# Expert gathers that begin per chunk of heads, dots ahead of the last selections, and a deeper ring of one-hot tiles

## The reference

```
q    = x @ w_q                       # 8 heads x 2 halves x 128
sc   = q . subkeys                   # 128 scores for each head and half
s_top, i_top = top16(sc)             # for each half
c_top, c_idx = top16(s_top[0][:,None] + s_top[1][None,:])   # 16 of 256 candidates
e1, e2  = i_top[0][c_idx // 16], i_top[1][c_idx % 16]
experts = e1 * 128 + e2              # 128 experts a token (8 heads x 16)
gates   = softmax(c_top)
h = sum_d x[d] * u_tab[experts, d]   # one row of 2048 for each token and expert
a = gates * gelu(h)
y = sum_k a[k] * v_tab[experts[k]]
```

## Time and profile before

| | |
|---|---|
| median of three runs | 2531.74 us (2524.23 to 2532.64) |
| the profiled execution's own time | 2534.31 us |
| its span, first to last instruction | 2532.5 us |
| busy share of the span | PE 70%, DVE 70%, ACT 35%, POOL 45% |
| indirect gathers L535 | 256, 2015 ns mean on POOL |
| dots L1243 | 256, 2288 ns mean |

### The profile page before, as it was taken

How to read it: one execution, slowest core, us unless ns; L and a number is a source line. 1 busy time by engine, 2 the same in 40 slices (tenths; PEclk the granted TensorE clock), 3 DMA queues, 4 the chain that set the end, 5 groups by cost and what they waited for, 6 DMA issues and landing times.

```text
span 2532.5 us, 24956 instructions
## 1 busy us (share of the span) xinstructions
PE 1760.8 (70%) x9462; PEld 1439.9 (57%) x9462; DVE 1762.5 (70%) x2424; ACT 877.8 (35%) x1369; POOL 1140.5 (45%) x484
## 2 busy tenths in 40 slices
PE   7997899899969630000130222799999999999798
PEld 6875778787769510000030222677777777777676
DVE  1066232422147799999999998798988899987714
ACT  3223122223222110000290794644444444444332
POOL 3662233335636266688777885022222222221154
PEclk9998899999979765555555555899999999999899
DMA  9997999987999398899999998299999899998547
GB/s 355 382 377 269 378 412 399 403 350 290 377 333 356 124 402 348 349 422 422 421 401 385 422 422 333 89 384 385 388 380 381 319 373 384 382 382 304 208 182 257
DMA packets 131558, 881.86 MB, mean 348 GB/s; under 512 B 18962, under 2 KB 20562, under 8 KB 55540
## 3 DMA queue, kind: packets, MB, share of 16 engines
q1 hardware_dynamic: 76148, 477.65, 49.3%
q0 software_dynamic: 55296, 402.68, 39.5%
HBM read 871.28 MB, written 141.63 MB: 400 GB/s over the span
## 4 chain that ended last, share of the span: by engine, by line
PE 37%; DVE 25%; POOL 14%; DMA 10%; issue 10%; ACT 2%; SPq 0%; POOLq 0%; ACTq 0%; DVEq 0%
POOL expert_rows L535 11%; PE psum L1427 10%; PE psum L1429 10%; PE psum L1428 10%; DVE expert_rows L1243 9%; DMA v_raw<-in_peer_v 7%; DVE v_lo L1369 2%; POOL w_lo L521 2%; DVE expert_rows L1304 2%; DMA cache_part<-in_k_parts 2%; DMA expert_rows<-in_peer_u,experts 2%; PE psum L1586 1%; DVE x_tokens L1313 1%; PE psum L1442 1%; PE psum L1443 1%
## 5 line engine op out<-in xcount | busy, mean ns | idle before, releaser
L535 POOL DMA_INDIRECT expert_rows<-in_peer_u,experts x256 | 515.9, 2015 | 187.8 <-DVE expert_rows L1243 81.4
L1243 DVE SCALAR_TENSOR_TENSOR expert_rows<-expert_rows,x_tokens 128x2048 f32<-128x2048 f32 x256 | 577.9, 2288 | 31.8 <-DMA expert_rows<-in_peer_u,experts 30.8
L521 POOL TENSOR_TENSOR w_lo<-w_raw,w_hi 128x2048 fp32r<-128x2048 f32 x80 | 371.2, 4640 | 476.8 <-ACT w_hi L566 476.7
L1427 PE MATMUL psum<-v_hi,gate_matrix_hi 128*128 128x512 f32 x1024 | 405.4, 396 | 33.7 <-DVE v_lo L1369 33.3
L809 ACT ACTIVATE v_hi<-v_raw 128x1024 fp32r<-128x1024 f32 x256 | 271.4, 1060 | 400.6 <-DMA v_raw<-in_peer_v 299.2
L1429 PE MATMUL psum<-v_hi,gate_matrix_lo 128*128 128x512 f32 x1024 | 399.8, 390 | 0.0
L1428 PE MATMUL psum<-v_lo,gate_matrix_hi 128*128 128x512 f32 x1024 | 399.7, 390 | 0.0
L1369 DVE TENSOR_TENSOR v_lo<-v_raw,v_hi 128x1024 fp32r<-128x1024 f32 x256 | 310.1, 1220 | 77.9 <-ACT v_hi L809 77.5
L566 ACT ACTIVATE w_hi<-w_raw 128x2048 fp32r<-128x2048 f32 x80 | 153.1, 1914 | 364.6 <-PE psum L1429 273.8
L1427 PEld LDWEIGHTS psum<-v_hi,gate_matrix_hi 128*128 128x128 f32 x1024 | 192.5, 188 | 97.6 <-issue 35.6
L1706 PE MATMUL psum<-one_hot_first_gated,one_hot_second 128*128 128x128 f32 x384 | 88.1, 405 | 221.5 <-ACT one_hot_first_gated L739 210.3
(11 more groups left out here) (307 smaller groups left out, 3071.3 us busy)
## 6 DMA issues: line engine op xcount, KB each, us to landing
v_raw<-in_peer_v SPq DMA_DIRECT2D x256, 512.0 KB, 7.2
out<-in_state_attn_k SPq DMA_DIRECT2D x64, 1020.0 KB, 10.7
out<-in_state_attn_v SPq DMA_DIRECT2D x64, 1020.0 KB, 11.2
w_raw<-in_w_in SPq DMA_DIRECT2D x48, 1024.0 KB, 8.6
cache_part<-in_k_parts SPq DMA_DIRECT2D x40, 1024.0 KB, 9.9
cache_part<-in_v_parts SPq DMA_DIRECT2D x40, 1024.0 KB, 12.5
w_raw<-in_w_out SPq DMA_DIRECT2D x16, 1024.0 KB, 7.0
w_raw<-in_peer_wq SPq DMA_DIRECT2D x16, 1024.0 KB, 6.5
```

Of the source, the lines that this page charges most:

```text
L521: nc.gpsimd.tensor_tensor(l_, r_, h_.bitcast(f32), ALU.subtract).then_inc(w_lo_ready, 1)
L535: pool.indirect_dma_start(ring[n % NSLOT][:, :], None, u_tab, bass.IndirectOffsetOnAxis(idx_p[:, n // PAIRS, n % PAIRS:n % PAIRS + 1], 0)) ...
L1243: V.scalar_tensor_tensor(out=g, in0=g, scalar=1.0, in1=xt[:, t, :], op0=ALU.mult, op1=ALU.mult, accum_out=hdot[:, t, j:j + 1]).then_inc(u_ ...
L1427: MM(out, lh, rh, start=start, stop=False)
```

## The change

Five things change. (1) The expert numbers of t = 1 are written by `select(1, c)`, chunk by chunk, and POOL may start a chunk's gathers when that chunk is known; `idx_ok` now counts four chunks and then t = 2. The slots are turned by three, so the first four gathers use slots 3 to 6; the fifth waits for the end of the query projection. (2) Before the loop stand three selections of each tile; `select(1, 3)` stands behind dot 8, `top_experts(0, 1)` behind dot 16, `select(2, 3)` behind dot 32, `top_experts(1, 2)` behind dot 48. (3) ACT makes the query copies. (4) PE makes a chunk's scores behind the first piece of the next chunk instead of the second. (5) In the open build both kinds of one-hot tile have four buffers, and ACT and DVE work three groups ahead instead of two.

```diff
+    emov_l = at("one_hot_first_late", [128, 2, EG, NK], f32, 184 * KB)
+    esta_l = at("one_hot_second_late", [128, 2, EG, NK], f32, 188 * KB)
...
+        slot_of = lambda n: (n + DSLOT) % NSLOT
...
+        deep = lambda g: g >= GROUPS // 2
+
+        def firsts(g):
+            return (emov_l if deep(g) and g % 4 > 1 else emov)[:, g % 2, :, :]
+
+        def seconds(g):
+            if early(g):
+                return gm[:, EG * g:EG * g + EG, :]
+            return (esta_l if deep(g) and g % 4 > 1 else esta)[:, g % 2, :, :]
+
+        def hots_free(g):
+            if g >= GROUPS // 2 + 4:
+                return g - 3
+            return GROUPS // 2 if deep(g) else g - 1
...
             for n in range(2 * PAIRS):
-                if n == 0 or n == PAIRS:
-                    pool.wait_ge(idx_ok, n // PAIRS + 1)
+                if n < PAIRS and n % (2 * TOPK) == 0:
+                    pool.wait_ge(idx_ok, n // (2 * TOPK) + 1)
+                if n == PAIRS:
+                    pool.wait_ge(idx_ok, 5)
+                if n == NSLOT - DSLOT:
+                    pool.wait_ge(w_used, 80)
                 if n >= NSLOT:
                     pool.wait_ge(u_free, n - NSLOT + 1)
-                pool.indirect_dma_start(ring[n % NSLOT][:, :], None, u_tab,
+                pool.indirect_dma_start(ring[slot_of(n)][:, :], None, u_tab,
...
+            def query_copies(c):
+                act.wait_ge(w_used, 64 + 4 * (c + 1))
+                for j in range(4):
+                    m = A(qpt[:, 4 * c + j, :], PS[:, 4 * (c % 2) + j, 0:N], ACT.Copy)
+                m.then_inc(acc_free, 1)
+
             for c in range(4):
                 for k in range(PPC):
                     if c > 0 or k > 1:
                         hi(64 + c * PPC + k, k % 2)
+                    if k == 1 and c > 0:
+                        query_copies(c - 1)
                     if k == 2 and c > 0:
                         score_copy(2 * c - 2)
                         score_copy(2 * c - 1)
+            query_copies(3)
...
             for g in range(GROUPS // 2, GROUPS):
-                if g + 2 < GROUPS and not by_dve(g + 2) and not early(g + 2):
-                    one_hots(g + 2)
+                if g + 3 < GROUPS and not by_dve(g + 3) and not early(g + 3):
+                    one_hots(g + 3)
...
                 if t == 1:
                     V.memset(mx[:, 2:3], 0.0).then_inc(ch_ok, 1)
+                    e1, e2 = (esel_p[:, 0, q, 2 * c:2 * c + 2, :].rearrange("p h k -> p (h k)") for q in range(2))
+                    V.scalar_tensor_tensor(out=idx_p[:, 0, 2 * TOPK * c:2 * TOPK * (c + 1)], in0=e1, scalar=float(NK), in1=e2,
+                                           op0=ALU.mult, op1=ALU.add).then_inc(idx_ok, 1)
...
-            query_copies(0)
             select(1, 0)
-            query_copies(1)
             select(2, 0)
             select(1, 1)
-            query_copies(2)
+            select(2, 1)
             select(1, 2)
-            query_copies(3)
-            select(1, 3)
-            top_experts(0, 1)
+            select(2, 2)
...
-            after_dot = {1: {8: lambda: select(2, 1), 24: lambda: select(2, 2), 40: lambda: select(2, 3),
-                             56: lambda: top_experts(1, 2)},
+            after_dot = {1: {8: lambda: select(1, 3), 16: lambda: top_experts(0, 1), 32: lambda: select(2, 3),
+                             48: lambda: top_experts(1, 2)},
...
-            for g in range(GROUPS // 2, GROUPS + 2):
+            for g in range(GROUPS // 2, GROUPS + 3):
                 if g < GROUPS:
                     one_hots(g)
-                if g - 2 >= GROUPS // 2 and by_dve(g - 2):
-                    build_copy(g - 2)
+                if g - 3 >= GROUPS // 2 and by_dve(g - 3):
+                    build_copy(g - 3)
...
-                    if k == 1 and c > 0:
+                    if k == 0 and c > 0:
                         pe.wait_ge(acc_free, 16 + c)
                         peer_scores(2 * c - 2)
                         peer_scores(2 * c - 1)
```

More of the change, by code:

```diff
@@ L312, in decoder_step @@
         by_dve = lambda g: g >= GROUPS * 3 // 4 and g % 4 == 3
-        def second_one_hot(g, j):
-            return gm[:, EG * g + j, :] if early(g) else esta[:, g % 2, j, :]
+        deep = lambda g: g >= GROUPS // 2
[9 more added lines that the diff above has]
+            return GROUPS // 2 if deep(g) else g - 1
         out_tile = lambda t: xd2[0:TS, :] if t == 0 else xt2[:, t - 1, :]
@@ L717, in one_hots @@
                 elif g >= 2:
-                    act.wait_ge(ab_mm, g - 1)
+                    act.wait_ge(ab_mm, hots_free(g))
                 else:
@@ L721, in one_hots @@
                 for j in range(EG):
-                    m = A(second_one_hot(g, j), iota[:, :], ACT.Abs, bias=eT[:, n, 1, c0 + j:c0 + j + 1], scale=-1.0)
+                    m = A(seconds(g)[:, j, :], iota[:, :], ACT.Abs, bias=eT[:, n, 1, c0 + j:c0 + j + 1], scale=-1.0)
                 m.then_inc(act_step, 1)
@@ L725, in one_hots @@
                 act.wait_ge(act_step, links[0])
-                v = (gm[:, EG * g:EG * g + EG, :] if early(g) else esta[:, g % 2, :, :]).rearrange("p a c -> p (a c)")
+                v = seconds(g).rearrange("p a c -> p (a c)")
                 A(v, v, ACT.Relu, bias=1.0, scale=-1.0).then_inc(es_e if early(g) else es_a, 1)
@@ L1197, in top_experts @@
                 e1, e2 = (parts[:, q, 0:hn, :].rearrange("p h k -> p (h k)") for q in range(2))
-                o = idx_d[:, :] if t == 0 else idx_p[:, t - 1, :]
-                link(V.scalar_tensor_tensor(out=o, in0=e1, scalar=float(NK), in1=e2, op0=ALU.mult, op1=ALU.add))
+                if t != 1:
+                    o = idx_d[:, :] if t == 0 else idx_p[:, t - 1, :]
+                    link(V.scalar_tensor_tensor(out=o, in0=e1, scalar=float(NK), in1=e2, op0=ALU.mult, op1=ALU.add))
+                if t == 2:
+                    V.memset(mx[:, 0:1], 0.0).then_inc(idx_ok, 1)
                 if t > 0:
-                    V.memset(mx[:, 0:1], 0.0).then_inc(idx_ok, 1)
                     V.memset(mx[:, 1:2], 0.0).then_inc(e_ok, 1)
@@ L1220, in select @@
                     V.memset(mx[:, 2:3], 0.0).then_inc(ch_ok, 1)
-            def query_copies(c):
-                dve.wait_ge(w_used, 64 + 4 * (c + 1))
-                for j in range(4):
-                    m = V.tensor_scalar(qpt[:, 4 * c + j, :], PS[:, 4 * (c % 2) + j, 0:N], 1.0, None, ALU.mult)
-                m.then_inc(acc_free, 1)
-            query_copies(0)
+                    e1, e2 = (esel_p[:, 0, q, 2 * c:2 * c + 2, :].rearrange("p h k -> p (h k)") for q in range(2))
+                    V.scalar_tensor_tensor(out=idx_p[:, 0, 2 * TOPK * c:2 * TOPK * (c + 1)], in0=e1, scalar=float(NK), in1=e2,
+                                           op0=ALU.mult, op1=ALU.add).then_inc(idx_ok, 1)
             select(1, 0)
-            query_copies(1)
             select(2, 0)
             select(1, 1)
-            query_copies(2)
+            select(2, 1)
             select(1, 2)
-            query_copies(3)
-            select(1, 3)
-            top_experts(0, 1)
+            select(2, 2)
             def prompt_dot(t, j):
                 n = (t - 1) * PAIRS + j
-                g = ring[n % NSLOT][:, :]
-                dve.wait_ge(u_in[n % NSLOT], 16 * (n // NSLOT + 1))
+                g = ring[slot_of(n)][:, :]
+                dve.wait_ge(u_in[slot_of(n)], 16 * (n // NSLOT + 1))
                 V.scalar_tensor_tensor(out=g, in0=g, scalar=1.0, in1=xt[:, t, :], op0=ALU.mult, op1=ALU.mult,
@@ L1251, in one_hots @@
             def one_hots(g):
[L1253 removed]
+                n, c0 = g // (GROUPS // 2), EG * (g % (GROUPS // 2))
                 dve.wait_ge(aT_ok, n + 1)
[L1255 to L1256 removed]
+                dve.wait_ge(ab_mm, hots_free(g))
                 for j in range(EG):
                     c = c0 + j
[L1259 removed]
+                    m = V.tensor_scalar(firsts(g)[:, j, :], iota[:, :], eT[:, n, 0, c:c + 1], aT[:, c:c + 1], ALU.is_equal, ALU.mult)
                 m.then_inc(em_ok, 1)
@@ L1284, in _ @@
                         V.memset(mx[:, 1:2], 0.0).then_inc(pack_rd, 1)
-                    if j == 0:
+                    if t == 2 and j == 0:
                         dve.wait_ge(sc_ok, 10)
@@ L1705, in build @@
                 for j in range(EG):
-                    m = MM(PS[:, build_bank(g), j * NK:(j + 1) * NK], second_one_hot(g, j), emov[:, g % 2, j, :], start=True, stop=True)
+                    m = MM(PS[:, build_bank(g), j * NK:(j + 1) * NK], seconds(g)[:, j, :], firsts(g)[:, j, :], start=True, stop=True)
                 m.then_inc(ab_mm, 1)
```

10 lines of the change are left out of this document (3 added, 7 removed).

## The result

The changed kernel takes 2499.76 us in the median of four runs (2494.68 to 2505.43), the kernel before on the same chip 2532.19 (2524.23 to 2537.15): a ratio of 0.9861, 95% interval 0.9841 to 0.9881. On the scale of the 2531.74 given with the case that is 2496.5.

What follows compares the result with a forecast made beforehand. DVE's dots and selections set the pace until the last selection, then transfers bound the gather stage. Gains of 18.6 there and 4 in the open build, 22.6 us, gave 2511.7 profiled, 2509 as median; range 2497 to 2521.

Steps and rivals of the forecast that it cites:

- the 22.6: Whole kernel: predicted gain in us, 18.6 in the gather stage plus 4 in the open build.
- What sets the stage's end: Gather stage: when dots resume behind the last selection and how many gathers remain (986.3, 216 gathers); gain 18.6 us.
- Query copies, scores, last `low`, start of gathers: Projection: ACT's copies 1.9 us a chunk, first scores 766.0, last `low` ends near 839.7, four gathers out by 844.
- The early start of gathers: Gather stage: starting gathers early gains nothing in itself, for seven slots fill in 17.4 us.
- rival D: Gathers don't go out while DVE selects; 5.2 us of waiting and 2.7 of paced dots return: 2517; chance 0.06.
- The stretch beside `low`: Selections ahead of the loop: POOL's `low` products lengthen them by 21.5 us together, bounds nothing and 51.
- The build: Open build: four buffers let DVE and ACT run ahead, gaining 4 of ACT's 6.2 idle us; bounds 0 and 6.2.
- Embeddings at nothing: Gather loop: PE's embeddings move 27 us later, to about 962 to 970; cost nothing, or 6 us if behind 987.
- The lead of seven slots: Gather loop: slots hold 17.4 us of transfers, 16 dots eat 4.3, so each selection finds the ring nearly full.
- Rival B: `low` meets fewer operations, half the 21.5 us, and all 6.2 of the build come: 35 us, 2496; chance 0.13.
- The forecast's other reading of it: Selections beside `low`: every two-input operation met pays a full `low`, 30.6 us in all, gain 9 us smaller.

Runs made afterwards that it cites:

- The old order: Changed kernel, but four selections of t = 1, one of t = 2 and top_experts(0, 1) ahead of the loop again; ratio 0.9902 (0.9872 to 0.9931).

## Why the prediction was right and where it was off

The mechanism behind the sum held; two of its terms were mis-sized, and they make 11.0 of the 12.1 us by which the change gave more than the 22.6.

- **What sets the stage's end** (when dots resume behind the last selection, and how many gathers remain): right. 106.2 us from the first dot to the resumption (105.7 forecast), 557.5 from there to the last dot (558.9 forecast). The old order agrees: from the first selection its first dot is 7.9 us earlier, yet its stage is no shorter (775.9 against 772.4).
- **Query copies, scores, last `low`, start of gathers**: right within 0.6 us each (the forecast's 766.0 for the scores adds up to 765.85). ACT's copies hide as the forecast had it; put back on DVE, with the scores behind the second piece again, they cost 11.
- **The early start of gathers** gains nothing but a full ring at the first dot, priced 5.2 + 2.7 = 7.9 in rival D: 9.4 measured by holding the gathers back.
- **The stretch beside `low`** is the first term that was mis-sized: 21.5 in the sum, 16.0 measured. The row of before (18.7 over four selections; its terms give 18.8) was spread over the new order by laying `low` against whole selections. What counts is whether one of a few kinds of short instructions falls into a `low`: the first four selections were to lose 7.1, 5.4, 7.6 and 1.4 us and lost 6.7, 1.3, 4.8 and 3.2. A row for each held instruction would have bounded it better than the selections' sums.
- **The build** is the second: 4 in the sum, bounded by 6.2, 9.5 measured. The step that failed is "of ACT's 6.2 idle us I take 4": it looked at ACT alone. ACT's part came to 5.4 of its 6.2; another 4.1 came in groups 32 to 47, where ACT makes no one-hots and DVE waited for PE.
- **Embeddings at nothing**: right for this order (last copy 954.66, forecast 962 to 970). One dot ahead of the second selection waits 0.65 us for its row (963.49), where the forecast had no such wait. The run with selections farther apart shows rows late behind the write where no selection hides it.
- **The lead of seven slots** was misread. The step "each selection finds the ring nearly full, fills it, and the transfers stop" fails already in the kernel before: at its three selections among dots 0, 1 and 1 landed rows lay ahead of the dots, and the other slots were under way. The transfers stop since those run out before the restart. The step led to no number of the sum, but where it was used, on spacing, it gave the wrong sign.
- **Rival B's number**, 2496, is the measured one, and that is luck: of its 10.7 us of stretch 5.5 came, and the build gave 9.5 where B ended at 6.2.

Together: 22.6 + 6.6 in the stage (5.5 of it the stretch) + 5.5 in the build = 34.7. The other 3.9 of the profiled 38.6 are not the change's: the v stage took 743.3 us in that run and 750.1 when the same kernel ran again, 747.1 before.

The Trainium skill ("SBUF — State Buffer", section "SBUF: two separate sides") says that a GpSimd instruction that has the shared port pair keeps it until its end, and that a VectorE instruction with two SBUF inputs, or in a mode that uses both ports, waits for it. The trace agrees: the five waits end with a `low`, within 0.6 us. One of the two kinds, and the CAST, have a single input; in which mode they ran no row shows. The forecast's other reading of it, a full `low` for every two-input operation met (30.6 us), falls: one operation waits, and those behind it find the pair free.

## What to carry to other kernels

Where two engines hold each other up, lay instruction against instruction: it is a few short ones that pay, and which ones is a matter of phase, which repeats from run to run. Price a deeper ring on every engine that fills or empties it, stage by stage, not by the idle time of the one that looked idle. A piece of work between the consumers of a ring that lasts, with the restart behind it, longer than what the ring has under way stops the producer however far apart such pieces stand; cutting it into short pieces is worth more than moving it (17 us here, while no other place of the whole selections differed by more than some 4).

## What was not expected of the hardware

A TENSOR_SCALAR on 128x32 integers, one input and 0.18 us alone, waited as the two-input ones do: 2.53, 1.51 and 3.30 us beside POOL's products, while the top-8 searches beside them kept their times; a CAST of integers, 0.20 alone, waited too (2.08 and 2.88). And a selection of 15.4 us stopped the transfers for some 9 to 10 us even where dots had been waiting for rows just before and the whole ring was under way: from the selection's end to the next landing it takes 10 us.
